# Two of three modulation groups of layer 0 summed by GpSimd, in a two-layer hybrid backbone on one Trainium2 core

## Chip, cores and metric

The kernel is one program on one core of a Trainium2 chip. The metric is the device time of an execution in microseconds. The engines are called as the profile calls them: PE (TensorE matmul), PEld (its weight load), DVE (VectorE), ACT (ScalarE), POOL (GpSimd), SP (SyncE, which here only issues DMAs).

## The reference

Two layers, each with adaLN modulation, a combined input projection, three parallel mixers (Mamba-2, grouped attention, Hyena), an output projection and a SwiGLU. 256 latent tokens and 256 context tokens go through layer 0 together. What the change touches is the modulation:

```python
c_act = silu(c); cctx_act = silu(c_ctx)                       # (1, 1024) and (1024,)
mod   = c_act    @ w_mod[l] + b_mod[l]                        # 6 groups of 1024 columns
mod_c = cctx_act @ w_mod[l] + b_mod[l]
sh1, sc1, g1, sh2, sc2, g2 = split(mod, 6)
h  = rmsnorm(x, norm1_g) * (1 + sc1) + sh1
proj = h @ w_in[l]                                            # the input projection
x  = x + g1 * (mix(proj) @ w_out[l])
x  = x + g2 * swiglu(rmsnorm(x, norm2_g) * (1 + sc2) + sh2)
```

Groups 0 and 1 (sh1, sc1) are needed before the input projection. Groups 2, 3 and 4 of layer 0 (g1, sh2, sc2) are made during it: each is a product of two rows of 1024 activations (one for the latent stream, one for the context) with a 1024 x 1024 matrix, all in float32. Together they are MODS_IN = 3 groups from MODS_FIRST = 2 on.

## The kernel before

All matmuls with large weights are made in three parts from halves of float32 (hi x hi, hi x lo, lo x hi). SP loads weight pieces (512 KB) into a ring of RING = 4 buffers (`load_w`, `load_in`); ACT makes w_hi from w_raw (L1439), DVE makes w_lo = w_raw - w_hi (L1812), PE uses both and releases the buffer by `w_used`. SP loads piece s + 4 when PE is done with piece s.

The input projection of layer 0 has 30 pieces, s = 0 to 29. Every engine's program is written out in order of s. On PE, `at_piece(s)` stands ahead of piece s and `in_piece(s)` in its middle; between the projection's matmuls these hold the small ones of the Mamba mixer: from s = 12 on a head per piece (`cum_rows`, then L942 in `y_head`, which waits for DVE's product em, L2089 and L2090) and from s = 13 on the states (L1032, L1039). At the end of `in_piece(s)` stands `mods_at(s)`.

`mods_at` makes the three modulation groups. Each group has KD = 8 pieces of `w_mod` (128 rows x 1024 columns, 512 KB), so there are 24 pieces pc, which SP loads in turn into the two buffers of `m_raw` (`load_mod`, L473). `mod_rows(pc)` waits for the piece and multiplies it by the activations: four matmuls into four groups of 32 partitions, each 256 columns of the piece, with `cact[:, k, :]` (32 columns, of which two are used) as the stationary operand; each float32 matmul has two records in the profile. The eight pieces of a group accumulate in PSUM bank MOD. MOD_AT puts two pieces each at s = 4, 6, ..., 26. When a group is done, ACT copies the bank to `m_row` (`copy_row`) and PE turns it into columns (`turn_row`, L656) at s = 12, 20 and 28 (`in_turn_at`).

SP loads modulation pieces 0 and 1 once the first groups' buffers are free; piece pc from 2 on is issued behind the weight load of s = MOD_AT[pc - 2] + RING and waits until PE has used piece pc - 2. Later groups (group 5 of layer 0 and those of layer 1) are made in the FFN of layer 0: DVE multiplies and adds the pieces into `m_acc` (128 partitions x 2 x 1024), and PE sums over the partitions with `m_pick` as the stationary operand, a matrix of zeros with one column of ones for each of the two rows (`summed_rows`, L646). DVE sets `m_pick` at the beginning of the output projection (L2285 to L2287).

GpSimd has only the split of the small `wdt` weights in each layer (L601, L603).

Of the kernel before, what the change touches and what calls it, by code (L numbers as in the profile page):

```python
# [14 lines left out]
ALU = mybir.AluOpType  # L15
# [7 lines left out]
KD = D // P  # L23
# [7 lines left out]
CW = 256  # L31
# [20 lines left out]
RING = 4  # L52
# [39 lines left out]

MOD_COLS = D
MODS_FIRST, MODS_IN = 2, 3
MOD_AT = [s for s in range(4, 28, 2) for _ in range(2)]
LAST_TURN = 28
SINE_LOADS, TAP_LOADS = 6, 3

MOD_SUMS, SUM_GROUPS = 8, 7
# [78 lines left out]

def in_turn_at(s):

    if s == LAST_TURN:
        return MODS_FIRST + MODS_IN - 1
    return next((m for m in range(MODS_FIRST, MODS_FIRST + MODS_IN - 1) if MOD_AT[8 * (m - 1)] == s), None)


def in_source(s):
# [49 lines left out]
def backbone(nc, x, c, ctx_in, c_ctx, w_mod, b_mod, norm1_g, w_in, ssd_conv_w, ssd_conv_b, ssd_a_log,  # L236
# [3 lines left out]
    with ExitStack() as stack:  # L240
# [14 lines left out]
        m_raw = at("m_raw", 80, [2, 4 * CW])  # L255
# [33 lines left out]
        wdts = [at(f"wdt{l}", kb, [8, 16]) for l, kb in enumerate((154, 176))]  # L289
        wdt_hl = at("wdt_hl", 201.5, [8, 32], F32R)  # L290
# [3 lines left out]
        cact = at("cact", 204, [KD, 32])  # L294
# [21 lines left out]
                           for name, off, shape in (("t_arg", 0, [L]), ("t_k", 1, [L]), ("t_h", 2, [2, L])))  # L316
        t_w1, t_w2, t_feats = at("t_w1", 168, [HD]), at("t_w2", 168.25, [HD]), at("t_feats", 168.5, [L])
        t_mask = at("t_mask", 169.5, [2, P])
        m_acc, m_pick = at("m_acc", 152, [2, MOD_COLS]), at("m_pick", 205, [2, 32])
        m_first = [at(f"m_first{m}", kb, [2, MOD_COLS]) for m, kb in enumerate((80, 112, 120, 128, 136, 88, 96, 104))]  # L320
        x_nat = at("x_nat", 16, [4, D])
        stag = at("stag", 32, [DEPTH, 2, P])
# [17 lines left out]
        ps = stack.enter_context(nc.psum_tensor("ps", [P, 8, 512], F32))  # L340
        MOD, STAT, ACC = 4, 5, 5
# [7 lines left out]
        mod_done = sem("mod_done")  # L349
        m_full = [sem("m_full0"), sem("m_full1")]  # L350
        m_used = sem("m_used")
        sq_full, consts_full, x_full = sem("sq_full"), sem("consts_full"), sem("x_full")
        small_full, hyw_full, sine_full = sem("small_full"), sem("hyw_full"), sem("sine_full")
        late_full = sem("late_full")
        wdt_full, wdt_hi_done, wdt_split = sem("wdt_full"), sem("wdt_hi_done"), sem("wdt_split")
        out_stored = sem("out_stored")
        conv_init = sem("conv_init")
        S = {name: sem(name) for name in (
# [87 lines left out]
        def _(sp):  # L446
# [20 lines left out]
            def load_mod(pc):  # L467


                if pc >= 2:  # L470
                    sp.wait_ge(m_used, pc - 1)
                k, c0 = pc % KD, (MODS_FIRST + pc // KD) * MOD_COLS
                sp.dma_start(m_raw[:, pc % 2, :], w_mod[0][k * P:(k + 1) * P, c0:c0 + MOD_COLS]).then_inc(m_full[pc % 2], 16)  # L473

            def load_big(j):


                sp.wait_ge(m_used, KD * MODS_IN)
                if j >= 2:
                    sp.wait_ge(S["mod_added"], mod_adds(j - 1))  # L480
                k0 = 2 * (j % 4)
                lm, group = divmod(MODS_FIRST + MODS_IN + j // 4, 6)
                c0 = group * MOD_COLS
                sp.dma_start(m_big[j % 2][:].rearrange("p (k n) -> p k n", n=MOD_COLS),
                             w_mod[lm].rearrange("(k p) n -> p k n", p=P)[:, k0:k0 + 2, c0:c0 + MOD_COLS]).then_inc(m_full[j % 2], 16)
# [55 lines left out]
            for l in range(DEPTH):  # L541
                for s in range(30):
                    if s >= RING or l > 0:
                        load_in(l, s)
                    if l == 0 and s == RING + 1:
                        sp.wait_ge(mod_done, KD + 1)
                        load_mod(0)
                        load_mod(1)
                    if l == 0 and s >= RING:
                        for pc in range(2, KD * MODS_IN):  # L550
                            if MOD_AT[pc - 2] == s - RING:
                                load_mod(pc)
                g = PLAN[l, "out"][0]
                src = w_out[l].rearrange("(k p) n -> p k n", p=P)
                turned = w_out[l][512:1024].rearrange("(j b e) n -> j e b n", j=2, e=HD)
                for s in range(12):
                    cols = slice((s % 4) * CW, (s % 4 + 1) * CW)
                    if s < PARTS:
                        k0 = 8 * (s // 4)
                        load_w(g + s, src[:, k0:k0 + 4, cols], 4)  # L560
                    else:
                        load_turned(g + s, turned[:, :, :, cols])
                    if l == 0 and s < 2:
                        for pc in range(2, KD * MODS_IN):
                            if MOD_AT[pc - 2] == 30 - RING + s:
                                load_mod(pc)
                for part, (c0, n) in enumerate(FFN):
                    g = PLAN[l, f"gu{part}"][0]
                    src = w_gu[l].rearrange("(k p) n -> p k n", p=P)
                    for s in range(4 * n):  # L570
                        up, half = gate_up(part, s // 4, s % 4)
                        col = up * DFF + (c0 + s // 4) * CW
                        load_w(g + s, src[:, 4 * half:4 * half + 4, col:col + CW], 4)
                        if l == 0 and mod_sum_at(ffn_slot(part, s)) is not None:
                            load_big(mod_sum_at(ffn_slot(part, s)))
                        if l == 0 and part == 1 and s == 1:
                            sp.wait_ge(S["rows_made"], 3)
                            load_sines(1, hyw_full)
# [15 lines left out]

        @block.gpsimd
        def _(pool):
            for l in range(DEPTH):
                pool.wait_ge(wdt_full, 16 * (l + 1))
                if l > 0:
                    pool.wait_ge(S["dt_psum"], l)  # L600
                nc.gpsimd.tensor_copy(wdt_hl[:, :, 0:16], wdts[l][:]).then_inc(wdt_hi_done, 1)  # L601
                pool.wait_ge(wdt_hi_done, l + 1)
                nc.gpsimd.tensor_tensor(wdt_hl[:, :, 16:32], wdts[l][:], wdt_hl[:, :, 0:16].bitcast(F32), ALU.subtract).then_inc(wdt_split, 1)  # L603


        @block.tensor
        def _(pe):
            mm, transpose = nc.tensor.matmul, nc.tensor.transpose
            p = Program(pe, "pe")
# [20 lines left out]
            def mod_rows(pc):  # L630


                pe.wait_ge(m_full[pc % 2], 16 * (pc // 2 + 1))
                k = pc % KD
                for g in range(4):
                    last = mm(ps[32 * g:32 * g + 32, MOD, CW:2 * CW], cact[:, k, :], m_raw[:, pc % 2, g * CW:(g + 1) * CW],
                              start=(k == 0), stop=(k == KD - 1))
                last.then_inc(m_used, 1)

            def summed_rows(m):  # L640
# [196 lines left out]
            for k in range(KD):  # L837
# [19 lines left out]
            for l in range(DEPTH):  # L857
# [187 lines left out]
                def mods_at(s):  # L1045

                    if in_turn_at(s) is not None:
                        turn_row(in_turn_at(s))
                    for pc in range(KD * MODS_IN):
                        if MOD_AT[pc] == s:  # L1050
                            mod_rows(pc)

                g0, q0 = PLAN[l, "in"]
                h_pair(g0, q0, T, l == 0)
# [307 lines left out]
        def _(act):  # L1362
# [60 lines left out]

            def copy_row(m):

                if m < MODS_FIRST + MODS_IN:
                    act.wait_ge(m_used, KD * (m - MODS_FIRST + 1))
                else:
                    p.after("rows_made")
                if m > MODS_FIRST:  # L1430
                    p.after("row_turned")
                p.sig(A(m_row[:], ps[:, MOD, CW:2 * CW], ACT.Copy), "row_ready")
# [340 lines left out]
        def _(dve):  # L1773
# [143 lines left out]
            for l in range(DEPTH):  # L1917
# [364 lines left out]

                split_w(g0 + 2)
                if l == 0:
                    p.chain(V.memset(m_pick[:], 0.0))  # L2285
                    p.link(V.memset(m_pick[:, 0, 0:1], 1.0))
                    p.link(V.memset(m_pick[:, 1, 1:2], 1.0))  # L2287
                    p.settle()
                    scale_mod(0, 1)
                if l == 0:  # L2290
                    part_residual(0)
# [225 lines left out]
```

## Time and profile before

| | us |
|---|---|
| median of 3 runs | 1243.56 (1243.14 to 1244.09) |
| profiled execution, its own time | 1244.54 |
| its span | 1242.7 |
| PE busy | 1202.8 (97%) |
| PEld busy | 962.6 (77%) |
| DVE busy | 821.6 (66%) |
| ACT busy | 523.6 (42%) |
| POOL busy | 1.7 |

The profile is of one execution. The span runs from its first instruction to its last, and 1.8 us lie around it. Busy shares are averages over stages of different kinds. "Idle before" names, for a group of instructions, the time in which the engine stood before them, and what ended it.

### The profile page before, as it was taken

Reading aid. Unit: us, or ns where it says so; the run is one execution under the profiler, and the core shown is the slowest. Engines: PE = TensorE matmul, PEld = TensorE weight load, DVE = VectorE, ACT = ScalarE, POOL = GpSimd, SP = SyncE. Lnnn points to the kernel's source line nnn. Section 1 sums busy time; section 2 is a strip of 40 time slices with the busy share of each in tenths; the row PEclk is TensorE's granted clock in tenths of the full one; section 3 lists DMA queues with packets and bytes.
Section 4 is the critical chain, followed back from the end, with each engine's and each line's share of the span. In section 5 each row is a group of like instructions: output and inputs, shape, how many; then the busy total and the mean of one; then the engine's idle time right before and its main releaser. Section 6 shows DMA issues by size and latency. Waiting matters only on the chain. (4 is left out here: it accounts for less than half of the span.)

```text
span 1242.7 us, 16729 instructions
## 1 busy us (share of the span) xinstructions
PE 1202.8 (97%) x6774; PEld 962.6 (77%) x6774; DVE 821.6 (66%) x1287; ACT 523.6 (42%) x907; POOL 1.7 (0%) x8
## 2 busy tenths in 40 slices
PE   5999999999999999999999999999998999999998
PEld 3666877777676788888887778778888778889888
DVE  4664357868766646767646656566589876776674
ACT  4362445442544433222222222357576454443454
POOL 0000000000000000000000000000000000000000
PEclk8999999999999999999999999999999999999999
DMA  9733242432011145554575454323344223655653
GB/s 336 247 123 105 93 162 86 157 99 65 18 35 40 63 138 201 195 194 166 192 230 172 168 178 169 94 62 95 114 119 119 69 52 119 187 185 187 187 177 128
DMA packets 132388, 171.82 MB, mean 138 GB/s; under 512 B 9268, under 2 KB 112342, under 8 KB 132312
## 3 DMA queue, kind: packets, MB, share of 16 engines
q1 hardware_dynamic: 131828, 170.58, 42.5%
q8 instruction: 53, 0.87, 0.3%
q10 hardware_dynamic: 484, 0.18, 0.1%
q14 instruction: 23, 0.19, 0.0%
HBM read 169.69 MB, written 1.05 MB: 137 GB/s over the span
## 5 line engine op out<-in xcount | busy, mean ns | idle before, releaser
L1812 DVE TENSOR_TENSOR w_lo<-w_raw,w_hi 128x1024 fp32r<-128x1024 f32 (+1 forms) x220 | 263.9, 1204 | 174.6 <-ACT w_hi L1439 172.6
L1439 ACT ACTIVATE w_hi<-w_raw 128x1024 fp32r<-128x1024 f32 (+1 forms) x220 | 228.3, 1042 | 332.0 <-DMA w_raw<-in_w_gu_dram 143.7
L700 PE MATMUL ps<-h_hi,w_hi 128*128 128x512 f32 (+1 forms) x576 | 218.7, 380 | 0.9 <-DVE w_lo L1812 0.6
L702 PE MATMUL ps<-h_hi,w_lo 128*128 128x512 f32 (+1 forms) x576 | 212.7, 369 | 0.0
L701 PE MATMUL ps<-h_lo,w_hi 128*128 128x512 f32 (+1 forms) x576 | 212.4, 369 | 0.0
L700 PE MATMUL ps<-f_hi,w_hi 128*128 128x512 f32 (+1 forms) x472 | 167.7, 355 | 4.2 <-DVE att_lo L2362 2.7
L702 PE MATMUL ps<-f_hi,w_lo 128*128 128x512 f32 (+1 forms) x472 | 162.5, 344 | 0.0
L700 PEld LDWEIGHTS ps<-h_hi,w_hi 128*128 128x128 f32 x576 | 108.5, 188 | 26.9 <-issue 8.8
L702 PEld LDWEIGHTS ps<-h_hi,w_lo 128*128 128x128 f32 x576 | 108.5, 188 | 18.8
L701 PEld LDWEIGHTS ps<-h_lo,w_hi 128*128 128x128 f32 x576 | 108.6, 189 | 17.4
L711 PE MATMUL ps<-h_hi,w_hi 128*128 128x512 f32 x320 | 113.2, 399 | 0.4 <-ACT gate L1744 0.4
L700 PEld LDWEIGHTS ps<-f_hi,w_hi 128*128 128x128 f32 x472 | 89.2, 189 | 21.3 <-issue 5.9
L702 PEld LDWEIGHTS ps<-f_hi,w_lo 128*128 128x128 f32 x472 | 89.2, 189 | 11.0
L701 PE MATMUL ps<-f_lo,w_hi 128*128 128x512 f32 (+1 forms) x240 | 90.1, 375 | 0.0
L712 PE MATMUL ps<-h_hi,w_lo 128*128 128x256 f32 x320 | 89.9, 281 | 0.0
L711 PEld LDWEIGHTS ps<-h_hi,w_hi 128*128 128x128 f32 x320 | 60.1, 188 | 15.4 <-DVE w_lo L1812 0.6
L712 PEld LDWEIGHTS ps<-h_hi,w_lo 128*128 128x128 f32 x320 | 60.5, 189 | 0.0
L701 PEld LDWEIGHTS ps<-f_lo,w_hi 128*128 128x128 f32 x240 | 45.2, 188 | 8.2 <-issue 0.5
L2431 DVE SCALAR_TENSOR_TENSOR m_acc<-m_odd,cact,m_acc 128x1024 f32<-128x1024 f32 x40 | 50.2, 1281 | 0.5
L1628 ACT ACTIVATE prob<-ps,sm 128x512 f32<-128x512 f32 (+1 forms) x48 | 29.1, 611 | 40.4 <-DVE sm L2255 37.9
L2394 DVE TENSOR_TENSOR hidden<-gate,ps 128x1024 f32<-128x1024 f32 (+1 forms) x12 | 14.1, 1176 | 41.9 <-PE ps L702 38.4
L1091 PE MATMUL ps<-w_hi,h_hi 128*128 128x512 f32 x96 | 40.8, 425 | 0.5 <-DVE xbc L1984 0.5
(342 smaller groups left out, 1910.0 us busy)
## 6 DMA issues: line engine op xcount, KB each, us to landing
w_raw<-in_w_gu_dram SPq DMA_DIRECT2D x88, 512.0 KB, 3.5
w_raw<-in_w_in_dram SPq DMA_DIRECT2D x60, 512.0 KB, 3.7
w_raw<-in_w_down_dram SPq DMA_DIRECT2D x32, 512.0 KB, 3.5
m_even<-in_w_mod_dram SPq DMA_DIRECT2D x14, 1024.0 KB, 5.9
m_odd<-in_w_mod_dram SPq DMA_DIRECT2D x14, 1024.0 KB, 5.8
m_raw<-in_w_mod_dram SPq DMA_DIRECT2D x24, 512.0 KB, 5.3
m_first<-in_w_mod_dram SPq DMA_DIRECT2D x16, 512.0 KB, 10.5
w_raw<-in_w_out_dram SPq DMA_DIRECT2D x16, 512.0 KB, 3.4
```

Of the source, the lines that this page charges most:

```text
L700: mm(o, w_hi[:, i % RING, w], hi[:, 0:n], start=first and k == 0, stop=False)
L701: mm(o, w_hi[:, i % RING, w], lo[:, 0:n], start=False, stop=False)
L702: last = mm(o, w_lo[:, i % RING, w], hi[:, 0:n], start=False, stop=final and k == nk - 1)
L711: mm(o, w_hi[:, i % RING, w], both(k), start=first and k == 0, stop=False)
L712: last = mm(o[:, 0:L], w_lo[:, i % RING, w], both(k)[:, 0:L], start=False, stop=final and k == nk - 1)
L1091: mm(o, h_hi[:, b, tok], w_hi[:, (i + half) % RING, w], start=(b == 0), stop=False)
L1439: A(w_hi[:, i % RING, w], w_raw[:, i % RING, w], ACT.Copy).then_inc(w_hi_done, 1)
L1628: p.sig(A(prob[:, i % 2, j, 0:keys], ps[:, 4 + j, 0:keys], ACT.Exp, bias=sm[:, 0, c:c + 1], accum_out=sm[:, 1, c:c + 1]), "probs_ready")
L1812: TT(w_lo[:, i % RING, w], w_raw[:, i % RING, w], w_hi[:, i % RING, w].bitcast(F32), ALU.subtract).then_inc(w_lo_done, 1)
L2394: TT(hidden[:, :, 0:n], gate[:, :, 0:n], ps[:, 2 * ((q + 1) % 2):2 * ((q + 1) % 2) + 2, 0:n], ALU.mult).then_inc(pair_free[(q + 1) % 2], 1)
L2431: ins = STT(out=acc, in0=src, scalar=by, in1=acc, op0=ALU.mult, op1=ALU.add)
```

## The change

Groups 2 and 3 (POOL_MODS = 2, so 16 pieces) are summed by GpSimd, group 4 stays with PE. For every piece and both streams s, GpSimd multiplies the piece (128 x 1024) by the activation of each partition (a column of `cact`) and adds the product to `p_acc[m]`; the first piece of a group is multiplied straight into `p_acc[m]`. Every one of these instructions waits for the one before it by the counter `pool_done`. It starts when PE has done the first groups (`mod_done` at 16) and waits for each piece. PE then sums over the partitions with `m_pick`, as for the later groups: `pool_summed_rows`, 8 matmuls of 128 x 256, at s = 11 and s = 17, after waiting for all 30 instructions of the group. The turns are at s = 12, 18 and 26. The eight pieces of group 4 are multiplied by PE two each at s = 18, 20, 22 and 24.

SP issues pieces 2 to 15 behind the weight loads of s = RING + (3, 3, 4, 5, 6, 7, 8, 9, 10, 10, 11, 12, 13, 14), and each waits until GpSimd has made the products of the piece two before. Pieces 16 and 17 come behind those of RING + 16 and 17, pieces 18 to 23 two each behind RING + 18, 20 and 22.

`m_pick` lies elsewhere and is set by GpSimd at its beginning. `wdt_hi_done` is merged into `pool_done`.

```diff
-MOD_AT = [s for s in range(4, 28, 2) for _ in range(2)]
-LAST_TURN = 28
+POOL_MODS, POOL_SET = 2, 4
+POOL_AT = [2 + 7 * pc // 8 for pc in range(8 * POOL_MODS)]
+ROWS_AT, TURN_AT = (11, 17), (12, 18, 26)
+MOD_AT = [s for s in range(18, 26, 2) for _ in range(2)]
...
+def pool_sums(m):
+
+    return POOL_SET + 30 * m
+
+
+def pool_products(pc):
+
+    m, k = divmod(pc, KD)
+    return pool_sums(m) + (2 if k == 0 else 4 * k + 1)
+
+
+def mod_load_at(pc):
+
+    if pc < 8 * POOL_MODS:
+        return POOL_AT[pc - 2] + 1
+    return (16, 17)[pc - 8 * POOL_MODS] if pc < 8 * POOL_MODS + 2 else MOD_AT[pc - 8 * POOL_MODS - 2]
...
                 if pc >= 2:
-                    sp.wait_ge(m_used, pc - 1)
+                    sp.wait_ge(pool_done, pool_products(min(KD * POOL_MODS, pc - 1) - 1))
+                if pc >= KD * POOL_MODS + 2:
+                    sp.wait_ge(m_used, POOL_MODS + pc - KD * POOL_MODS - 1)
...
+            def sum_mods(m):
+
+                pool.wait_ge(mod_done, 2 * KD)
+                if m == 1:
+                    pool.wait_ge(S["taps_ready"], 1)
+                for k in range(KD):
+                    pc = KD * m + k
+                    pool.wait_ge(m_full[pc % 2], 16 * (pc // 2 + 1))
+                    for s in range(2):
+                        acc, by = p_acc[m][:, s, :], cact[:, k, s:s + 1]
+                        if k > 0:
+                            pool.wait_ge(pool_done, pool_products(pc) - 3 + 2 * s)
+                        nc.gpsimd.tensor_scalar(acc if k == 0 else p_part[:], m_raw[:, pc % 2, :], by, None,
+                                                ALU.mult).then_inc(pool_done, 1)
+                        if k > 0:
+                            pool.wait_ge(pool_done, pool_products(pc) - 2 + 2 * s)
+                            nc.gpsimd.tensor_tensor(acc, acc, p_part[:], ALU.add).then_inc(pool_done, 1)
+                pool.wait_ge(pool_done, pool_sums(m + 1))
...
+            def pool_summed_rows(m):
+
+                pe.wait_ge(pool_done, pool_sums(m + 1))
+                for s in range(2):
+                    for g in range(4):
+                        last = mm(ps[32 * g:32 * g + 32, MOD, CW:2 * CW], m_pick[:, s, :], p_acc[m][:, s, g * CW:(g + 1) * CW],
+                                  start=(s == 0), stop=(s == 1))
                 last.then_inc(m_used, 1)
...
                     if in_turn_at(s) is not None:
                         turn_row(in_turn_at(s))
-                    for pc in range(KD * MODS_IN):
-                        if MOD_AT[pc] == s:
-                            mod_rows(pc)
+                    if s in ROWS_AT:
+                        pool_summed_rows(ROWS_AT.index(s))
+                    for j, at_s in enumerate(MOD_AT):
+                        if at_s == s:
+                            mod_rows(KD * POOL_MODS + j)
...
                 if l == 0:
-                    p.chain(V.memset(m_pick[:], 0.0))
-                    p.link(V.memset(m_pick[:, 0, 0:1], 1.0))
-                    p.link(V.memset(m_pick[:, 1, 1:2], 1.0))
-                    p.settle()
                     scale_mod(0, 1)
```

## Rows read from the trace of the kernel before

**Rows 1.** The page, busy us (share of the span) and instructions.

```profile
PE 1202.8 (97%) x6774; PEld 962.6 (77%) x6774; DVE 821.6 (66%) x1287; ACT 523.6 (42%) x907; POOL 1.7 (0%) x8
```

**Rows 2.** Stretches: their length, busy us of each engine (instructions), clock, DMA share, GB/s.

```profile
60.00:100.00 40.00, 39.84 (x224) 26.94 (x224) 21.90 (x41) 21.95 (x32) 0.00 (x0) 1.00 0.38 122
...
140.00:180.00 40.00, 40.00 (x262) 31.71 (x261) 21.20 (x33) 19.23 (x54) 0.00 (x0) 1.00 0.32 106
...
220.00:260.00 40.00, 40.00 (x220) 31.12 (x219) 34.76 (x65) 21.27 (x51) 0.00 (x0) 1.00 0.43 141
```

**Rows 3.** PE's waits, 40 to 290 us: total us, times, longest.

```profile
PE ps L1039 <- DVE ysum L2019: 0.9, 1, 0.9
PE ps L892 <- issue: 0.8, 1, 0.8
...
PE ps L700 <- DVE xbc L1984: 0.2, 1, 0.2
```

**Rows 4.** The tile m_raw on PE: duration ns min/median/max, first and last start.

```profile
L636 PE MATMUL ps<-m_raw,cact x192: 379/379/403, 67.7 to 255.0; 128*32 128x256 f32 x192
```

**Rows 5.** PE in order of time around one pair: start us, busy us, line, matmul.

```profile
67.12 0.39 PE L701 MATMUL ps<-h_lo,w_hi 128*128 128x512 f32 x1
67.35 0.39 PE L702 MATMUL ps<-h_hi,w_lo 128*128 128x512 f32 x1
67.67 1.07 PE L636 MATMUL ps<-m_raw,cact 128*32 128x256 f32 x16
...
69.01 0.40 PE L701 MATMUL ps<-h_lo,w_hi 128*128 128x512 f32 x1
```

**Rows 6.** The tile m_pick on DVE.

```profile
L2285 DVE MEMSET m_pick<- x1: 112/112/112, 285.3 to 285.3; 128x64 f32 x1
```

**Rows 7.** All groups of POOL: count, busy us, mean ns; then idle time before them.

```profile
L603 POOL TENSOR_TENSOR wdt_hl<-wdt,wdt_hl 128x128 fp32r<-128x128 f32 x2 | 0.9, 462 | 0.2
L601 POOL CAST wdt_hl<-wdt 128x128 fp32r<-128x128 f32 x2 | 0.6, 292 | 624.4 <-DMA wdt<-in_w_in_dram 624.4
...
L2506 POOL MEMSET const-float32-1.0<- 128x1 f32 x1 | 0.1, 98 | 0.0
```

**Rows 8.** Groups of DVE, 57 to 185 us, same columns.

```profile
L1812 DVE TENSOR_TENSOR w_lo<-w_raw,w_hi 128x1024 fp32r<-128x1024 f32 x15 | 18.3, 1221 | 11.6 <-ACT w_hi L1439 11.5
...
L2089 DVE TENSOR_TENSOR em<-em 128x512 f32<-128x512 f32 x6 | 4.2, 692 | 8.2 <-ACT em L1570 8.2
...
L2079 DVE TENSOR_TENSOR xw<-xsn,wst 128x512 f32<-128x512 f32 x4 | 2.7, 684 | 0.0
...
L2035 DVE TENSOR_TENSOR dt<-dt,dtr 128x64 f32<-128x64 f32 x1 | 0.2, 226 | 0.6 <-ACT dt L1534 0.6
```

**Rows 9.** SP's queue in order of time: start us, us, line, DMA.

```profile
49.69 1.20 SPq L473 DMA_DIRECT2D m_raw<-in_w_mod_dram  x2
...
126.90 0.38 SPq L515 DMA_DIRECT2D w_raw<-in_w_in_dram  x1
...
135.89 0.38 SPq L515 DMA_DIRECT2D w_raw<-in_w_in_dram  x1
...
151.70 0.38 SPq L515 DMA_DIRECT2D w_raw<-in_w_in_dram  x1
...
162.57 0.38 SPq L451 DMA_DIRECT2D w_raw<-in_w_in_dram  x1
```

**Rows 10.** PE in order of time, pieces 15 and 17.

```profile
163.34 1.00 PE L942 MATMUL ps<-xsn,em 128*128 128x64 f32 x8
...
184.65 1.02 PE L1032 MATMUL ps<-xw,bnat 128*128 128x256 f32 x4
```

**Rows 11.** DMAs of m_raw, us to landing: issued before 60 us.

```profile
DMA to landing us min/median/max: 8.8/9.1/9.5
```

**Rows 12.** The same, 60 to 120 us.

```profile
DMA to landing us min/median/max: 4.5/5.1/5.7
```

**Rows 13.** DVE in order of time, one em.

```profile
159.58 0.69 DVE L2090 TENSOR_TENSOR em<-em,gT 128x512 f32<-128x512 f32 x1
```

More of the change, by code:

```diff
@@ L179, in in_turn_at @@
 def in_turn_at(s):
-    if s == LAST_TURN:
-        return MODS_FIRST + MODS_IN - 1
-    return next((m for m in range(MODS_FIRST, MODS_FIRST + MODS_IN - 1) if MOD_AT[8 * (m - 1)] == s), None)
+    return MODS_FIRST + TURN_AT.index(s) if s in TURN_AT else None
+def pool_sums(m):
[7 more added lines that the diff above has]
+    return (16, 17)[pc - 8 * POOL_MODS] if pc < 8 * POOL_MODS + 2 else MOD_AT[pc - 8 * POOL_MODS - 2]
 def in_source(s):
@@ L318, in backbone @@
         t_mask = at("t_mask", 169.5, [2, P])
-        m_acc, m_pick = at("m_acc", 152, [2, MOD_COLS]), at("m_pick", 205, [2, 32])
+        m_acc, m_pick = at("m_acc", 152, [2, MOD_COLS]), at("m_pick", 186.75, [2, 32])
+        p_acc = [at("p_acc0", 132, [2, MOD_COLS]), at("p_acc1", 104, [2, MOD_COLS])]
+        p_part = at("p_part", 120, [MOD_COLS])
         m_first = [at(f"m_first{m}", kb, [2, MOD_COLS]) for m, kb in enumerate((80, 112, 120, 128, 136, 88, 96, 104))]
@@ L354, in backbone @@
         late_full = sem("late_full")
-        wdt_full, wdt_hi_done, wdt_split = sem("wdt_full"), sem("wdt_hi_done"), sem("wdt_split")
+        wdt_full, wdt_split = sem("wdt_full"), sem("wdt_split")
+        pool_done = sem("pool_done")
         out_stored = sem("out_stored")
@@ L475, in load_big @@
             def load_big(j):
-                sp.wait_ge(m_used, KD * MODS_IN)
+                sp.wait_ge(m_used, POOL_MODS + KD * (MODS_IN - POOL_MODS))
                 if j >= 2:
@@ L550, in _ @@
                         for pc in range(2, KD * MODS_IN):
-                            if MOD_AT[pc - 2] == s - RING:
+                            if mod_load_at(pc) == s - RING:
                                 load_mod(pc)
@@ L562, in _ @@
                         load_turned(g + s, turned[:, :, :, cols])
[L563 to L566, printed above, removed]
                 for part, (c0, n) in enumerate(FFN):
@@ L596, in _ @@
         def _(pool):
+            def sum_mods(m):
[15 more added lines that the diff above has]
+                pool.wait_ge(pool_done, pool_sums(m + 1))
+            nc.gpsimd.memset(m_pick[:], 0.0).then_inc(pool_done, 1)
+            pool.wait_ge(pool_done, 1)
+            nc.gpsimd.memset(m_pick[:, 0, 0:1], 1.0).then_inc(pool_done, 1)
+            nc.gpsimd.memset(m_pick[:, 1, 1:2], 1.0).then_inc(pool_done, 1)
             for l in range(DEPTH):
@@ L600, in _ @@
                     pool.wait_ge(S["dt_psum"], l)
-                nc.gpsimd.tensor_copy(wdt_hl[:, :, 0:16], wdts[l][:]).then_inc(wdt_hi_done, 1)
-                pool.wait_ge(wdt_hi_done, l + 1)
+                nc.gpsimd.tensor_copy(wdt_hl[:, :, 0:16], wdts[l][:]).then_inc(pool_done, 1)
+                pool.wait_ge(pool_done, POOL_SET if l == 0 else pool_sums(POOL_MODS) + 1)
                 nc.gpsimd.tensor_tensor(wdt_hl[:, :, 16:32], wdts[l][:], wdt_hl[:, :, 0:16].bitcast(F32), ALU.subtract).then_inc(wdt_split, 1)
+                if l == 0:
+                    sum_mods(0)
+                    sum_mods(1)
         @block.tensor
@@ L637, in mod_rows @@
                               start=(k == 0), stop=(k == KD - 1))
+                last.then_inc(m_used, 1)
+            def pool_summed_rows(m):
[4 more added lines that the diff above has]
+                                  start=(s == 0), stop=(s == 1))
                 last.then_inc(m_used, 1)
@@ L1424, in copy_row @@
             def copy_row(m):
-                if m < MODS_FIRST + MODS_IN:
-                    act.wait_ge(m_used, KD * (m - MODS_FIRST + 1))
+                if m < MODS_FIRST + POOL_MODS:
+                    act.wait_ge(m_used, m - MODS_FIRST + 1)
+                elif m < MODS_FIRST + MODS_IN:
+                    act.wait_ge(m_used, POOL_MODS + KD * (m - MODS_FIRST - POOL_MODS + 1))
                 else:
```

## The prediction

> **What bounds the kernel now.** I read the page's busy shares first [rows 1]: PE is busy 1202.8 of 1242.7 us, POOL 1.7 us in all. Then the table by stretches [rows 2]: in the first layer's input projection, 60 to 260 us, stretches of 40 us have PE busy 39.84, 40.00 and 40.00 at full granted clock, DMA at 0.32 to 0.43, and DVE at 21.9, 21.2 and, after 220, 34.8. Then PE's waits from 40 to 290 us [rows 3]: the longest of six is 0.9 us (for DVE), the shortest 0.2. So in this stretch a matmul taken off PE is time taken off the kernel, as long as nobody else becomes late by as much.
>
> **What leaves PE.** The 24 weight pieces of the three groups are 192 records of 379 ns on PE, and they come in 12 pairs of 16 records [rows 4, 5]. What one pair costs is read from the start times around it [rows 5]: the last matmul ahead starts at 67.35, the second one behind at 69.01, which is 1.66 us; without the pair these are two steps of 0.23 us (67.12 to 67.35). So a pair costs 1.66 - 0.46 = 1.20 us, filling and draining included. The change removes eight pairs (at pieces 4 to 18 of the projection, since two groups of eight go), keeps four (now at 18, 20, 22, 24), and adds two readings of GpSimd's sums, each 2 rows x 4 column groups = 8 matmuls of 128x256 f32, the shape and number of one pair: 1.20 us each. PE: -8 x 1.20 + 2 x 1.20 = -7.2 us. The three turns of a row stay three. DVE loses three memsets of m_pick, the longest 0.11 us, at 285 us [rows 6]; GpSimd does them before its first wait, where it is idle. I cost both at nothing. The 24 DMAs of m_raw stay 24, with the same bytes.
>
> **What GpSimd needs.** A piece after the first of a group is two products and two additions over 128x1024, each waiting for the one before; the first is two products. The trace shows no such instruction on POOL. Nearest are its own two at 128x128 [rows 7]: 462 ns for two inputs, 292 ns for one, and 0.1 us between them (0.2 for both). Of the fixed part they say nothing; a memset of one column took 98 ns, and DVE's 128x64 took 226 ns against 692 for 128x512, a fixed part of 0.16 us [rows 8]. With 0.16 fixed: (462-160) x 8 + 160 = 2.58 us, (292-160) x 8 + 160 = 1.22 us, and a piece is 2 x (2.58 + 1.22) + 4 x 0.1 = 8.0 us. With 0.098 fixed: 3.01, 1.65 and 9.7 us, the upper end. At DVE's own speed for this shape, 1.22 us [rows 8], it is 5.3 us, the lower end. I take 8.0: it comes from POOL's own rows, and of the two fixed parts the larger is that of real two-input work, where a memset of one column reads nothing. The Trainium skill (GPSIMD Engine Reference, section 3.1) gives 4497 ns for a two-input add of 2048 and about 2.6 cycles an element, thus an estimate of some 2.3 us here, and with 1.2 for a product a piece near 7.4 us; no row here shows it, and by it the last piece would end near 174, with the sum the same.
>
> **Is it in time?** Two walls: PE reads the first sum in the middle of piece 11, the second in the middle of piece 17, and being in order it stands there if POOL is late, with all the projection behind it. The trace of before has these places near 131.4 (between the weight loads that the ends of pieces 10 and 11 release, 126.90 and 135.89) and at 185.7 (end of L1032, 184.65 + 1.02) [rows 9, 10]. Four pairs less move the first to 126.6; seven less and one reading more move the second by 7.2 to 178.5. POOL starts when the first piece has landed: issued at 49.69, 9.1 us [rows 11], so 59.0. The loads are issued behind the weight loads of SP's queue and land 5.1 us later [rows 12]. The first sum: two products (2.6), then seven pieces of 8.0, end about 118. That is 9 us before its wall. In the second the loads hold it: the last three pieces are tied to three weight loads, the first issued at 151.70, the last at 162.57 [rows 9], earlier now by 4.8 and 6.0 (four and five pairs net); the first of the three has landed at 152.3, and 3 x 8.0 end at 176.3. That is 2.2 us before the wall. So at 8.0 a piece nothing is late; the wall is hit from 8.2 a piece (59.0 + 5.2 + 14 pieces = 178.5); the gain is gone when POOL is 7.2 us late, at 8.7. At 9.7 all: 59.0 + 6.6 + 135.8 = 201.4, 22.9 us late.
>
> SP's queue: each m_raw load now waits for POOL's products of two pieces before, and stands in front of the next weight load. At 8.0 a piece it holds SP some 5 us once (second pair of loads, 62 to 67), else about 1. Weight loads are issued four pieces ahead, some 30 us; after DMA (5 us at most), ACT's copy and DVE's 1.2 us more than 20 us are left. Nothing. ACT's copy of a row waits for PE's reading, which stands one piece before it: nothing either.
>
> **DVE beside a busy POOL.** The trace never has both at work on large tiles, so its cost is bounded: nothing below, since no DVE work is removed in this stretch; above, the case under "rivals". DVE's own slack towards PE is small from piece 13: its product em is done at 160.27 (159.58 + 0.69) and PE reads it at 163.34, 3.1 us later [rows 10, 13]. I take 1.5 us in all, as a late second sum or one or two late em.
>
> The sum: profiled execution 1244.54 (span 1242.7, 1.8 around it), median of the runs 1243.56. 1244.54 - 7.2 + 1.5 = 1238.8; taken to the median, **1237.9**. Does the saving survive after piece 17? From 220 to 260 us DVE is at 34.8 of 40 while PE shows 40.0 [rows 2]; the saving is made before 178, when DVE is half idle and waits for PE or ACT, and of PE's waits on DVE the longest is 0.9 us [rows 3]. With 5 us of DVE idle in those 40, at worst 3 to 4 of the 7.2 come back as waits.
>
> **Rivals.**
> 1. POOL is late at the second wall by more than 7.2 us, and the kernel is slower. For it: the other reading of the two POOL rows (9.7 a piece), giving 22.9 late, 1243.6 - 7.2 + 22.9 = 1259. A second mechanism to the same wall is the port: if a POOL instruction and a DVE one with two inputs can't run together, DVE's w_lo (15 x 1.22 = 18.3), em (two lines of 4.2) and xw (2.7) between 57 and 185 us [rows 8] push POOL by 29 us; 59.0 + 5.2 + 112 + 29 = 205, 26.7 us late, 1263. Against: POOL's two rows run over strips of 16 elements, which may have made them dearer than long ones, and no row shows such exclusion. It decides from 8.7 a piece, collisions included. The Trainium skill (SBUF — State Buffer, section Who interferes with whom) says just this: a DVE instruction with two SBUF inputs and a GpSimd one that reads SBUF exclude each other, and the second blocks until the first ends. The trace can't confirm it, POOL being idle beside those DVE rows. Chance 0.24.
> 2. DVE is the one that waits: PE's reading of em and of the states from piece 13 to 17 stalls. Each of five pieces has two em instructions in chain that could each wait behind a POOL addition of 2.6 us, 5.2 in place of 3.1 of slack: 5 x 2.1 = 10.5 at the most, half of it likely. 1243.6 - 7.2 + 5.2 = 1241.6. For it: the chain of waits between DVE and PE there; against: only POOL instructions under way count. Chance 0.12.
> 3. The gain is made and half lost after 220 us to DVE: 1240.5 to 1241. Chance 0.06.
> 4. The change takes its whole PE term, and no more: that is the forecast, 1236.4 to 1240, chance 0.58.
>
> **How the numbers follow.** What a measurement tells from no change is about 0.2%, 2.5 us: 1241.1 and 1246.0. Faster: the forecast 0.56, half of rivals 2 and 3, 0.07, together 0.63. Same: the rest of these and the small latenesses of rival 1 (POOL 5 to 9 us late), 0.13. Slower: 0.24. The range starts at 1235.5, a pair at a little over 1.20 and nothing lost, and reaches to 1253, POOL 16 us late, where about 1 in 10 of the chance lies above. The likeliest case's own range is 1235.5 to 1241.
>
> **What would show it.** Right: 128 fewer records for L636 and 32 new ones for m_pick with p_acc; POOL busy some 110 us between 59 and about 176 us, with additions near 2.6 and products near 1.2 us; no PE wait on POOL at either reading; the place of piece 26 7 us earlier. Wrong: a PE wait on POOL at piece 17 (rival 1), w_lo and em longer than 1.22 and 0.69 us or PE waits on em (rival 2), PE waits on DVE after 220 us (rival 3). The forecast falls if a piece takes POOL more than 8.7 us.

## The result, and the profile after

The changed kernel takes 1299.18 us (1297.75 to 1299.84, 4 runs), the kernel before 1243.35: ratio 1.0457 (1.0443 to 1.0470), 55.8 us slower. The forecast was 1237.9, the range ended at 1253. It was wrong in sign and size. The profiled execution has a span of 1296.0 us, against 1242.7 before.

The stretches that answer to [rows 2], same columns:

```profile
60.00:100.00 40.00, 34.82 (x172) 24.59 (x171) 30.07 (x38) 18.38 (x29) 38.53 (x15) 0.96 0.28 88
100.00:140.00 40.00, 32.70 (x122) 22.32 (x122) 20.85 (x16) 8.88 (x11) 38.61 (x14) 0.87 0.27 93
140.00:180.00 40.00, 30.38 (x185) 23.52 (x183) 16.99 (x18) 14.88 (x37) 38.35 (x14) 0.91 0.28 92
180.00:220.00 40.00, 32.14 (x122) 23.95 (x120) 18.58 (x20) 10.76 (x33) 38.51 (x15) 0.83 0.28 92
220.00:260.00 40.00, 23.40 (x126) 17.32 (x127) 18.47 (x25) 9.25 (x23) 16.03 (x6) 0.79 0.25 79
260.00:300.00 40.00, 39.15 (x217) 30.37 (x216) 34.38 (x76) 21.79 (x59) 0.00 (x0) 1.00 0.37 119
```

In each row POOL's busy time stands last of the five engines: it is busy 38.5 of every 40 us, almost without a gap, from 57 to 237 us, and PE has holes for just as long. PE's granted clock is lower in the stretches with long waits (0.83 and 0.79 from 180 to 260; it was 1.00 before). The groups of POOL, answering to [rows 7]:

```profile
L628 POOL TENSOR_SCALAR p_part<-m_raw,cact 128x1024 f32<-128x1024 f32 x28 | 90.3, 3225 | 4.1 <-POOL p_acc L632 2.4 <-POOL p_acc L628 0.3
L632 POOL TENSOR_TENSOR p_acc<-p_acc,p_part 128x1024 f32<-128x1024 f32 x28 | 70.0, 2500 | 2.3
```

The additions take the 2.5 us of the forecast. The products, which have one input tile less, take 3.2. DVE is slowed too: w_lo took 1221 ns before [rows 8], and between 57 and 238 us now

```profile
L1870 DVE TENSOR_TENSOR w_lo<-w_raw,w_hi 128x1024 fp32r<-128x1024 f32 x16 | 38.6, 2411 | 33.5 <-ACT w_hi L1497 33.4
```

PE's waits (40 to 270 us), answering to [rows 3], and the two readings of GpSimd's sums:

```profile
PE ps L690 <- POOL p_acc L632: 23.3, 2, 18.0
PE ps L946 <- issue: 6.1, 1, 6.1
PE ps L996 <- DVE ysum L2168: 5.1, 2, 2.7
```

```profile
L690 PE MATMUL ps<-p_acc,m_pick x32: 634/634/636, 146.9 to 237.9; 128*32 128x256 f32 x32
```

```profile
236.60 1.94 PE L690 MATMUL ps<-p_acc,m_pick 128*32 128x256 f32 x16 [17.96 <-POOL p_acc L632]
```

The second reading begins at 236.60; its place before was 185.7 [rows 10]. That is 50.9 of the 53.3 us by which the two profiled spans differ. What lies behind that place took 1242.7 - 185.7 = 1057.0 us of the span before and 1296.0 - 236.6 = 1059.4 now, 2.4 more: the reading itself (1.94), and matmuls at the lower clock after the wait (634 ns a record in place of 379; granted clock 0.64 from 236 to 243 us), less one pair at the end.

The wait that the profile names is only 23.3 us. The rest of the 50.9 shows as waits for something else. SP's queue, answering to [rows 9], is locked to POOL:

```profile
85.23 0.33 SPq L496 DMA_DIRECT2D m_raw<-in_w_mod_dram  x1
85.60 0.43 SPq L538 DMA_DIRECT2D w_raw<-in_w_in_dram  x1
97.00 0.33 SPq L496 DMA_DIRECT2D m_raw<-in_w_mod_dram  x1
97.37 0.43 SPq L538 DMA_DIRECT2D w_raw<-in_w_in_dram  x1
108.77 0.33 SPq L496 DMA_DIRECT2D m_raw<-in_w_mod_dram  x1
```

A weight load leaves every 11.8 us, right behind a load that waited for POOL. ACT's waits for weights, 40 to 360 us (23.6 us in the kernel before):

```profile
ACT w_hi L1497 <- DMA w_raw<-in_w_in_dram: 77.6, 15, 10.4
```

It looks as if SP were the cause. So three theories went into the experiments. A: POOL's chain is too long for PE's second reading, and all waits before it are only other places for the same delay. B: weight loads held back behind GpSimd. C: DVE and GpSimd get in each other's way.

### The profile page after: what moved, and what is told of

It reads as the page before. It is cut to its first block and busy times, and to the rows that moved or that the text cites. A ratio compares the mean times of both kernels' runs of the same rounds, so it can differ in the third digit from the quotient of the medians.

```text
span 1296.0 us, 16619 instructions
## 1 busy us (share of the span) xinstructions
PE 1211.6 (93%) x6678; PEld 970.6 (75%) x6678; DVE 853.2 (66%) x1284; ACT 523.6 (40%) x907; POOL 174.4 (13%) x71
## 5 line engine op out<-in xcount | busy, mean ns | idle before, releaser
L1870 DVE TENSOR_TENSOR w_lo<-w_raw,w_hi 128x1024 fp32r<-128x1024 f32 (+1 forms) x220 | 283.0, 1290 | 194.2 <-ACT w_hi L1497 192.1
L628 POOL TENSOR_SCALAR p_part<-m_raw,cact 128x1024 f32<-128x1024 f32 x28 | 90.3, 3225 | 4.1 <-POOL p_acc L632 2.4
L632 POOL TENSOR_TENSOR p_acc<-p_acc,p_part 128x1024 f32<-128x1024 f32 x28 | 70.0, 2500 | 2.3
```

The source lines that it names most:

```text
L628: nc.gpsimd.tensor_scalar(acc if k == 0 else p_part[:], m_raw[:, pc % 2, :], by, None, ALU.mult).then_inc(pool_done, 1)
L632: nc.gpsimd.tensor_tensor(acc, acc, p_part[:], ALU.add).then_inc(pool_done, 1)
L1870: TT(w_lo[:, i % RING, w], w_raw[:, i % RING, w], w_hi[:, i % RING, w].bitcast(F32), ALU.subtract).then_inc(w_lo_done, 1)
```

## Experiments

Ratios are against the kernel before, run beside each batch (its medians 1240.9 to 1242.2). "Reading" is the start of the second (or only) reading in the profile. e2 has one run, 1246.3 us, and serves for its instructions alone.

| | median us | ratio (95%) | reading |
|---|---|---|---|
| e1 mixture beside | 1251.7 | 1.0090 (1.0069 to 1.0111) | |
| e3 half width | 1242.2 | 1.0010 (1.0000 to 1.0019) | 184.0 |
| e4 own loads | 1301.1 | 1.0475 (1.0457 to 1.0493) | 239.5 |
| e5 704 columns | 1255.7 | 1.0117 (1.0093 to 1.0141) | 192.3 |
| e6 later reading | 1283.7 | 1.0339 (1.0320 to 1.0358) | 241.5 |
| e7 two-input products | 1270.0 | 1.0235 (1.0210 to 1.0260) | 209.0 |
| e8 memsets beside | 1240.7 | 0.9985 (0.9975 to 0.9995) | |
| e9 one group early | 1260.9 | 1.0162 (1.0134 to 1.0190) | 153.3 |
| e10 one group late | 1264.6 | 1.0188 (1.0173 to 1.0204) | 218.8 |
| e11 beside, after the filter | 1246.4 | 1.0045 (1.0029 to 1.0060) | |
| e12 both mends | 1271.7 | 1.0252 (1.0235 to 1.0269) | 227.3 |
| e13 one-input beside | 1243.5 | 1.0014 (1.0004 to 1.0024) | |
| e14 two-input beside | 1277.6 | 1.0287 (1.0270 to 1.0303) | |
| e15 one group, one-input | 1251.1 | 1.0073 (1.0061 to 1.0086) | 151.2 |

### e1: the same work beside the kernel before

```diff
+                for _ in range(12):
+                    for s in range(2):
+                        nc.gpsimd.tensor_scalar(b_part[:], src, cact[:, 0, s:s + 1], None, ALU.mult).then_inc(beside_done, 1)
...
+                        nc.gpsimd.tensor_tensor(b_part[:], b_part[:], src, ALU.add).then_inc(beside_done, 1)
```

> The kernel before, with GpSimd doing 12 pieces' worth of the same instructions (48: products 128x1024 from a constant table, additions into a scratch tile, each waiting for the one before) from 46 us on, for which nobody waits; its results are used nowhere. Theory A (the length of GpSimd's own chain is the cause, through PE's readings at pieces 11 and 17): collisions with DVE alone cost little, 1243 to 1248 us. Theory C (the collisions of DVE and GpSimd are the cause): over 12 of 16 pieces some three quarters of the loss, 1275 us or more. In both POOL's instructions last what they last in the changed kernel, 2.85 and 2.4 us, more where DVE's w_lo is under way, and w_lo is longer than 1.22 us.

10.7 us more than before: between the two. Nobody waits for POOL here, so this is what the collisions (times in which DVE and GpSimd keep each other waiting) cost by way of DVE, three quarters of the work for a fifth of the loss. It refutes C as the main cause, and my 1.5 us for collisions too. What they cost by making POOL's own instructions longer can't show here; it is part of A, and is worked out in the section on the prediction.

Where the time goes is read from the start of the same matmuls in both traces. PE is 3.5 us ahead of the kernel before at 47 us (up to there profiles of these kernels differ by up to 4 us), 0.5 behind at 60, 2.2 behind at 100, 6.1 behind from 108, and 6.5 from 150 on. So 4.0 of the 10.0 us are lost before 60 us, where the changed kernel's POOL has hardly begun, 3.9 at one place in the filter, and only 0.4 between 112 and 190 us, though POOL is as busy there.

### e2: what a product costs

The same place, four of each kind:

```diff
+ nc.gpsimd.tensor_scalar(b_part[:], src, by, None, ALU.mult)                      # and over 512
+ nc.gpsimd.tensor_scalar(b_part[:], src, 2.0, None, ALU.mult)
+ nc.gpsimd.tensor_copy(b_part[:], src)
+ nc.gpsimd.tensor_tensor(b_part[:], src, src, ALU.add)                            # and over 512
+ nc.gpsimd.tensor_tensor(b_part[:], src, by.to_broadcast([P, MOD_COLS]), ALU.mult)
```

> The kernel before with 28 GpSimd instructions beside it, four of each kind, for which nobody waits: product by a column of scalars over 1024 and over 512, product by a constant, copy, addition of two tiles over 1024 and 512, and a product written as two-input instruction. What a product's 2.84 us are made of: if it is the fetching of the scalars, the constant one is near 1.2 us; if it is the instruction's rate, the constant one is 2.8 us too, the one over 512 1.4 to 1.5 us, and a two-input product 2.4 us.

One line each: duration ns min/median/max.

```profile
L608 POOL TENSOR_SCALAR b_part<-c_fwd,cact x4: 2846/2999/3089, 45.2 to 54.4; 128x1024 f32<-128x1024 f32 x4
L613 POOL TENSOR_SCALAR b_part<-c_fwd,cact x4: 1562/1566/2863, 57.5 to 63.8; 128x512 f32<-128x512 f32 x4
L618 POOL TENSOR_SCALAR b_part<-c_fwd x4: 2770/2772/2822, 65.5 to 74.1; 128x1024 f32<-128x1024 f32 x4
L623 POOL COPY b_part<-c_fwd x4: 1037/1040/1043, 76.9 to 80.2; 128x1024 f32<-128x1024 f32 x4
L628 POOL TENSOR_TENSOR b_part<-c_fwd x4: 1892/1892/2753, 81.4 to 88.1; 128x1024 f32<-128x1024 f32 x4
L638 POOL TENSOR_TENSOR b_part<-c_fwd,cact x4: 1893/1893/1894, 95.4 to 101.3; 128x1024 f32<-128x1024 f32 x4
```

It is the instruction's own rate: a constant as multiplier changes 2.85 to 2.77, half the width 1.56. A copy takes 1.04. The copy is where my 1.22 for "one input" belongs; a product by a scalar is 2.7 times as long, and longer than the two-input form that does the same (1.89, where I had expected 2.4).

### e3 and e5: fewer columns

```diff
-                        acc, by = p_acc[m][:, s, :], cact[:, k, s:s + 1]
+                        n = slice(0, MOD_COLS if k == 0 else 512)      # e5: 704
+                        acc, by = p_acc[m][:, s, n], cact[:, k, s:s + 1]
```

> The changed kernel with every GpSimd product and addition after the first piece of a group over 512 of the 1024 columns (the sums of the other columns are left out of the result). A piece takes POOL about 5.9 us instead of 11.8, faster than the loads come. Theory A: no wait at either reading, and the forecast of 1236 to 1241 us comes true. Theory C: with half the time in which both are at work, half the loss stays: 1260 us or more. Theory B (SP's queue is held by GpSimd): like A, since the products come in time.

> The changed kernel with GpSimd's products and additions after the first piece of a group over 704 of 1024 columns (the sums of the others are left out of the result). From the half and whole widths a piece takes POOL about 8.5 us, near the 8.0 of the forecast and beyond its wall of 8.2. Theory A (PE's second reading is tied to the end of GpSimd's chain, and the time is that moment plus what follows it): chain 57 + 12 + 14 x 8.5 = 188, the rest as in the changed kernel (1299 - 237 = 1062): about 1250 us. If collisions with DVE are the cause and not the wall: half-way between the half width (1242) and the whole (1299) or above, 1263 us or more.

e3: 1242.2, no wait at a reading (the second begins at 183.96, 1.7 before its old place), so A's first half holds, but the gain that it foretold is missing. e5: 1255.7 for A's 1250 (the chain ended at 192, not 188), below C's 1263. PE's second reading waited:

```profile
192.31 1.93 PE L691 MATMUL ps<-p_acc,m_pick 128*32 128x256 f32 x16 [6.45 <-POOL p_acc L633]
```

What lies behind the reading hardly differs in the profiled spans: 1243.1 - 184.0 = 1059.1 in e3, 1252.9 - 192.3 = 1060.6 in e5, 1059.4 in the changed kernel. So the loss lies ahead of the reading at all three widths, and the wait at it follows the end of POOL's chain: none, 6.5, 18.0 us. That is A.

Where e3's gain went is read from PE's rows. Across a place without waits the change does what it should. L1032 to L922 of the kernel before, with a pair between, and L1087 to L977 of e3, without:

```profile
157.57 1.02 PE L1032 MATMUL ps<-xw,bnat 128*128 128x256 f32 x4
...
162.47 0.50 PE L922 MATMUL ps<-csr,pick 40*128 40x512 f32 x2
```

```profile
157.89 1.02 PE L1087 MATMUL ps<-xw,bnat 128*128 128x256 f32 x4
...
161.61 0.50 PE L977 MATMUL ps<-csr,pick 40*128 40x512 f32 x2
```

4.90 against 3.72: 1.18 for a pair, as forecast (1.20). But PE waits for DVE in the filter at 102 to 105 us. L947 is the first matmul that needs the filter's sums t_sum and t_diff; the profile names no releaser ("issue"), but the program makes PE wait there for DVE's signal that they are ready:

```profile
PE ps L947 <- issue: 2.8, 1, 2.8
PE ps L1094 <- DVE ysum L2078: 0.9, 1, 0.9
PE ps L934 <- DVE t_filt L2106: 0.7, 1, 0.7
```

The place itself, in e3 and then in the kernel before:

```profile
105.35 3.65 PE L947 MATMUL ps<-t_sum,c_fwd 128*128 128x512 f32 x4 [2.82 <-issue]
```

```profile
106.63 1.95 PE L892 MATMUL ps<-t_sum,c_fwd 128*128 128x512 f32 x4 [0.80 <-issue]
```

PE comes there 3.3 us earlier than before and leaves 0.4 later: 2.0 us more of waiting, and then the same four matmuls take 1.7 us longer, at a granted clock of 0.50 (106 to 108 us), the lower of its two levels, 1.2 in place of 2.4 GHz. So this one wait eats 3.7 of the 7.2 us. Not all of it is collisions: DVE's last sum ended at 105.25 against 106.53, with about 1.0 us of lengthened instructions between 99 and 105 us. Without these PE, being 3.3 us earlier, would still have had to wait.

### e4: loads issued by GpSimd

```diff
-                            if mod_load_at(pc) == s - RING:
+                            if pc >= KD * POOL_MODS and mod_load_at(pc) == s - RING:
...
+                        nc.gpsimd.dma_start(m_raw[:, nx % 2, :], w_mod[0][nk * P:(nk + 1) * P, c0:c0 + MOD_COLS]).then_inc(p_full[nx % 2], 16)
```

> The changed kernel with the loads of pieces 2 to 15 issued by GpSimd itself instead of SP, so that no weight load stands behind a wait for GpSimd. Theory B (SP's queue, held to GpSimd's pace, starves PE: ACT's waits for weight DMAs rose to 77.6 us): most of the loss goes, 1265 us or less. Theory A: PE only waits in another place, at the readings, some 5 + 45 us instead of 5 + 18, and the time stays between 1290 and 1302 us.

1301.1: B falls. PE now waits where the cause is:

```profile
PE ps L696 <- POOL p_acc L633: 44.3, 2, 33.0
```

33.0 in place of 18.0 us at the second reading, which begins at 239.46. ACT's waits for weights, 40 to 270 us, are back near the 23.6 us of before, and the time is not:

```profile
ACT w_hi L1503 <- DMA w_raw<-in_w_in_dram: 26.6, 7, 8.9
```

The 77.6 us were a symptom.

### e6: the second reading two pieces later

```diff
-ROWS_AT, TURN_AT = (11, 17), (12, 18, 26)
+ROWS_AT, TURN_AT = (11, 19), (12, 20, 28)
-MOD_AT = [s for s in range(18, 26, 2) for _ in range(2)]
+MOD_AT = [s for s in range(20, 28, 2) for _ in range(2)]
```

> The changed kernel with PE's second reading at piece 19 instead of 17 (turns at 20 and 28, the last group's pieces at 20 to 26), nothing else. Theory A: the reading comes at the same moment, 237 us, but PE has two more pieces behind it by then, 17 us: about 1282 us. Theory B (weight loads held to GpSimd's pace): PE can't use the room, since its weights come at GpSimd's pace until the products of piece 15: 1290 us or more.

1283.7: 15.5 us for A's 17. The weights, held to POOL's pace, did cost a little: the reading came at 241.5, 5 late, and without a wait of its own.

### e7, e9, e10, e12: two-input products, and one group only

e7 rewrites the product; e12 is e7 with e6's reading. e9 and e10 use e7's product and give GpSimd one group (POOL_MODS = 1).

```diff
-                        nc.gpsimd.tensor_scalar(acc if k == 0 else p_part[:], m_raw[:, pc % 2, :], by, None,
-                                                ALU.mult).then_inc(pool_done, 1)
+                        nc.gpsimd.tensor_tensor(acc if k == 0 else p_part[:], m_raw[:, pc % 2, :], by.to_broadcast([P, MOD_COLS]),
+                                                ALU.mult).then_inc(pool_done, 1)
```

> The changed kernel with GpSimd's product written as a two-input instruction, the activation broadcast along the row, 1.9 us instead of 2.84 where it was tried alone. A piece: 2 x (1.9 + 2.4) + 0.5, and some 0.7 of collisions, 9.8 us; chain 57 + 8 + 14 x 9.8 = 202, plus 1062: about 1264 us by theory A. If it is not the product's length but the number of instructions and waits, the time stays near 1299 us.

> One group only (group 2) on GpSimd, from 57 us on, products as two-input instructions, read by PE at piece 12; PE multiplies groups 3 and 4 two pieces each at pieces 13 to 27. PE's term is -4 x 1.2 + 1.2 = -3.6 us, and GpSimd's chain ends near 135 us, before the reading. If what is left of the loss is DVE's delay in the filter's chain (its products and sums from 80 to 112 us, for which PE waits), it costs the 4 to 6 us that it cost with half widths: 1242 to 1245 us. If collisions cost little beside a chain that is in time: 1238 to 1240 us.

> One group only (group 3) on GpSimd, from about 128 us on, behind the filter's chain; PE multiplies group 2 at pieces 4 to 10 as before and group 4 at 21 to 27, and reads GpSimd's sums at piece 19. Same term of PE, -3.6 us. If the collisions cost time only where the filter's chain runs, and GpSimd's chain of about 4 + 7 x 9.8 us ends at the reading (about 202 us): 1238 to 1240 us, faster than before. If they cost time beside the heads and states too, 1242 us or more.

> The changed kernel with both mends that helped: products as two-input instructions and the second reading at piece 19. Theory A: if the reading comes at 209 us as with the products alone, 209 + 1061 - 19 = 1251 us; what is left above the kernel before is GpSimd's length and the collisions. If the reading no longer waits: 1244 to 1248 us.

e7: 1270.0 with a reading at 209.0 (1268.3 - 209.0 = 1059.3 of the span behind it) seems to confirm A, but PE waited only 2.2 us there; it was late by itself. e12 shows it: the chain ends at 209.0 again, PE comes to the reading only at 227.3 and waits for nothing, and the time is 1271.7 and not 1251. And e9 and e10, with chains that end at 132.7 and 214.2 us, ahead of readings at 153.3 and 218.8, lose 20 and 24 us. e9 and e12 lie outside both of their branches, e10 in its open one (1242 or more), e7 6 us above; a second cause had been left out. PE's longest waits in e7 are two for DVE and the one in the filter (L946):

```profile
PE ps L1017 <- DVE adt L2094: 7.0, 1, 7.0
PE ps L946 <- issue: 6.6, 1, 6.6
PE ps L996 <- DVE em L2148: 5.2, 1, 5.2
```

and DVE's em, 692 ns before [rows 8], is mostly waiting:

```profile
L2148 DVE TENSOR_TENSOR em<-em,gT 128x512 f32<-128x512 f32 x7 | 15.7, 2244 | 0.2
```

### e8, e13, e14: which GpSimd instruction holds DVE up

e11 first: the mixture only from 130 us on.

> The kernel before with GpSimd doing 7 pieces' worth of products and additions, for which nobody waits, but only after the filter's chain, from about 130 us to 207 us. With 12 pieces from 46 us on it was 10.7 us slower. If those came from the filter's chain and the projection's beginning, 1241 to 1243 us; if they come evenly, 6 us more than before, 1247 us.

1246.4, 5.5 more for 7 pieces, 0.8 a piece; e1 had 0.9. So collisions cost time behind the filter too. But the like price a piece is chance: in this trace 4.8 us are lost at one wait of 3.3 us (L720, for DVE's qk, at 190.9), and e1 lost 0.4 us between 112 and 190. The cost comes in steps, where PE happens to wait for a short DVE chain.

```diff
+ nc.gpsimd.memset(b_part[:], 0.0)                                                     # e8, x108
+ nc.gpsimd.tensor_scalar(b_part[:], src, cact[:, 0, 0:1], None, ALU.mult)             # e13, x44
+ nc.gpsimd.tensor_tensor(b_part[:], src, cact[:, 0, 0:1].to_broadcast([P, MOD_COLS]), ALU.mult)   # e14, x60
```

> The kernel before with 108 GpSimd memsets of 128x1024 beside it, over the time of the 48 products and additions, nobody waits for them. They write SBUF and read nothing. If it is GpSimd's reading that excludes DVE's two-input instructions, w_lo stays at 1.22 us and the time at that of before, 1240 to 1243 us. If being busy or writing is enough, w_lo is longer again and the time is some 10 us more, as with products and additions.

> The kernel before with 44 one-input GpSimd products (2.85 us each, some 130 us in all) beside it from about 46 us on, nobody waits. Theory D (a one-input product keeps DVE's two-input instructions out only in its first microsecond, a two-input instruction for its whole length): w_lo near 1.3 us on average, the time 1241 to 1245 us. Rival (what counts is the share of time in which GpSimd is busy): 8 to 12 us more than before, as with 48 products and additions.

> The kernel before with 60 two-input GpSimd products (1.9 us each, lengthened by collisions to some 130 us) beside it over the same time, nobody waits. Theory D: DVE's two-input instructions wait behind nearly every one, w_lo 2 us or more, and the time is 15 us or more above before, beyond the 10.7 of the mixture. Rival: the same 8 to 12 us as with the other kinds.

w_lo between 57 and 185 us, in e8, e13 and e14 (before: 1221 ns, [rows 8]):

```profile
L1829 DVE TENSOR_TENSOR w_lo<-w_raw,w_hi 128x1024 fp32r<-128x1024 f32 x15 | 18.3, 1220 | 9.9 <-ACT w_hi L1454 9.8
```

```profile
L1829 DVE TENSOR_TENSOR w_lo<-w_raw,w_hi 128x1024 fp32r<-128x1024 f32 x15 | 21.3, 1422 | 9.9 <-ACT w_hi L1454 9.8
```

```profile
L1829 DVE TENSOR_TENSOR w_lo<-w_raw,w_hi 128x1024 fp32r<-128x1024 f32 x11 | 25.1, 2286 | 9.7 <-ACT w_hi L1454 9.6
```

Memsets cost nothing (103 us of them), 132 us of one-input products 1.4 us, 127 us of two-input ones 35.5 us. That is theory D for both kinds of product. The same seen singly in e1, POOL and then DVE:

```profile
67.89 2.85 POOL L607 TENSOR_SCALAR b_part<-c_fwd,cact 128x1024 f32<-128x1024 f32 x1
70.82 2.56 POOL L610 TENSOR_TENSOR b_part<-b_part,c_fwd 128x1024 f32<-128x1024 f32 x1
73.48 2.90 POOL L607 TENSOR_SCALAR b_part<-c_fwd,cact 128x1024 f32<-128x1024 f32 x1
```

```profile
69.93 1.22 DVE L1833 TENSOR_TENSOR w_lo<-w_raw,w_hi 128x1024 fp32r<-128x1024 f32 x1
71.06 2.47 DVE L2061 CAST maskb<-t_mask 128x256 bf16<-128x256 f32 x1
73.46 0.22 DVE L2062 CAST identb<-c_sq 128x128 bf16<-128x128 f32 x1
73.71 2.02 DVE L1833 TENSOR_TENSOR w_lo<-w_raw,w_hi 128x1024 fp32r<-128x1024 f32 x1
75.65 0.77 DVE L2046 TENSOR_SCALAR bc<-bc 128x32 f32<-128x32 f32 x1
```

The first w_lo begins 2.04 us into a product and runs as ever. The cast (0.29 us in the kernel before) begins inside an addition and ends when that has ended. The second w_lo begins 0.23 us into a product and is held some 0.8 us, until about 1.0 us of the product are over. Of the w_lo of e1 between 60 and 180 us, the seven that began 1.8 us or more into a product took 1.21 to 1.23 us.

The last row is an exception that theory D lacks: bc, with one input out of SBUF, took 0.18 us before; here it begins 2.17 us into a product and ends with it. In e8 such short ones wait for memsets as well:

```profile
70.03 0.80 DVE L2042 TENSOR_SCALAR bc<-bc 128x32 f32<-128x32 f32 x1
```

### e15: one group, one-input products

e9 with the products of the changed kernel, the reading one piece later (13) and the other groups' pieces at 14 to 28.

> One group only (group 2) on GpSimd from 57 us on, its products one-input instructions as in the changed kernel, read by PE at piece 13; groups 3 and 4 by PE, two pieces each, at pieces 14 to 28. PE's term -3.6 us. Theory D: the loss of e9 (20 us) came from its two-input products; here the collisions cost what they cost in the mixture for eight of twelve pieces, about 5 us, and the chain ends near 146 us, 0 to 3 us behind the reading: 1242 to 1248 us. If DVE's delay comes from the additions as much as from the products: 1255 us or more.

1251.1 (after 1260.9 in e9), between the two branches: product for product, the longer instruction is the better neighbour. It is still 9 us above before; the 14 additions remain, and PE waits 4.1 us at L949 for the filter. No version tried beats the kernel before. Whether one with fewer additions would, was not tried.

## Why the prediction was wrong

- **PE's term, right.** 1.18 us a pair where no wait interferes, and two readings. It never reached the end in any version. What the prediction left out is that PE, once earlier, meets DVE's filter chain, which doesn't get earlier by as much (e3).
- **What GpSimd needs: the step that failed.** "(292-160) x 8 + 160 = 1.22 us" takes a cast's row for a product by a scalar. The product takes 2.85 alone, 3.2 in place. A piece is 11.8 us (SP's rows: 85.23, 97.00, 108.77), not 8.0, and above the 9.7 that I had called the upper end: the bound was made of the same wrong row. The addition, 2.58, was right (2.34 at least, 2.50 on average). The chain ended at 236.5, 60.2 us behind the forecast's 176.3. By the rows, the 32 products at 2.85 in place of 1.22 are 52 us of it, the 28 additions at 2.34 in place of 2.58 give back 7, and what POOL's instructions took above their shortest times, beside DVE, is 16 us (172.5 busy in all).
- **Is it in time: the method was right.** With 11.8 a piece and the 12.1 us that the four products of the two first pieces took put into the same sum, 59.0 + 12.1 + 14 x 11.8 = 236.3, against 236.6 seen, and 178.5 as the wall gives 57.8 late and 1243.6 - 7.2 + 57.8 = 1294.2 for the measured 1299.2. The limit of 8.2 us a piece is only bracketed: e3 with about 6.7 waits for nothing, e5 with about 8.7 is 6.5 us late. The forecast's "Nothing" for SP's queue became false in the trace (ACT waits 77.6 us for weights), but e4 shows that this costs no time while PE's reading is the limit.
- **DVE beside a busy POOL: mis-sized.** I took 1.5 us. e1 measures 10.7 for 12 pieces (some 6 of it from 60 us on), and e3, with POOL in time at half the work, loses the whole gain, in part to collisions. In the changed kernel itself this term is hidden: PE waits for POOL anyway, and the collisions count by the 16 us that they add to POOL's chain. Rival 2 had the mechanism, but looked for it only at pieces 13 to 17; it acts wherever DVE has a short chain that PE waits for, first in the filter and the step sizes at 70 to 112 us. Nor did any term count that matmuls behind such a wait can run slower (1.7 us in e3). Here the Trainium skill's rule (SBUF — State Buffer, section Who interferes with whom), which the prediction left at 0.24 with the long chain, is borne out in direction: w_lo 1220 ns beside memsets, 2286 beside two-input reads. That the second blocks until the first ends holds for two-input instructions of GpSimd here, while beside a product of 2.85 us DVE's two-input instructions waited only for its first microsecond.
- **The rivals.** Rival 1 is what happened, with both of its halves, a dearer piece and DVE pushing POOL (16 us where it had 29): 1259 and 1263 by my sizes, 1299 measured. Its chance of 0.24 rested on a duration that no row supported in either direction.

## What to carry to other kernels

Take an instruction's price from a row of that very operation on that engine; if there is none, the upper bound must come from another kind of row, or the range must say it is open. Work that moves to an idle engine is paid twice: as a deadline (sum the chain with its loads and compare it with the moment of the reader), and as time in which it and a neighbouring engine keep each other out (here GpSimd and DVE), and the second can eat a gain even when the first is met. A wait put on PE can cost more than its length, since the matmuls behind it may run at the lower clock, as they did in e3 and in the changed kernel. In a trace, many long waits for a DMA or for another engine can be the shadow of one reader further on: remove the suspected cause, and see whether the end moves.

## What the runs showed of the hardware

- GpSimd, 128x1024 float32: memset 0.95 us, copy 1.04, product of a tile and a column written with two inputs 1.89, in-place addition 2.34, product as tensor with scalar 2.85 (constant 2.77; 128x512 1.56).
- A two-input GpSimd instruction and DVE's two-input ones (and small casts and scalar ones out of SBUF) excluded each other for the whole instruction. A GpSimd product by a scalar kept DVE's two-input ones out for about 1.0 of its 2.85 us, memsets did not at all. Short one-input ones out of SBUF could wait all the same: one that began 2.2 us into a product until its end (bc, 0.77 in place of 0.18 us in e1), and for memsets (0.80 in e8). It works both ways: in the changed kernel products of 2.85 us took 3.7 behind a w_lo.
- DVE's instructions that read PSUM beside SBUF (xbc, 746 ns against 749) were not lengthened.
- In PE's wait of 18 us before the second reading the granted clock was 0.50 (1.2 GHz) from 227 us, stayed there until 240, and was 1.00 again from 243; the reading ran at 634 ns a record in place of 379. In e3, behind a wait of 2.8 us, it was 0.50 from 106 to 108 us, and four matmuls took 3.65 us in place of 1.95.
